# Expert layer of a two-block transformer kernel: 80 candidate sums, eight one-hot places, four operand places, pairs loaded two at a time

## The reference, cut to what matters

```python
q = (h @ w_q).reshape(B, S, 8, 2, 128)
s1, s2 = q[..., 0, :] . keys1, q[..., 1, :] . keys2        # 128 scores each, per token and head
v1, i1 = top_k(s1, 16);  v2, i2 = top_k(s2, 16)
cand = (v1[..., :, None] + v2[..., None, :]).reshape(..., 256)
sv, si = top_k(cand, 16)
experts = i1[si // 16] * 128 + i2[si % 16]                 # 128 picks per token, of 16384 experts
gates = softmax(sv)
a = h . u[experts];  act = gelu(a) * gates;  out = sum over picks of act * v[experts]
x = x + out
```

## Time and profile before

| | us |
|---|---|
| three runs | 2755.32, 2766.57, 2768.15 (median 2766.57) |
| profiled execution, its own time | 2760.16 |
| span from its first to its last instruction | 2758.3 |
| PE busy / DVE / POOL / ACT in the span | 2562.9 / 1672.7 / 1799.8 / 727.3 |
| stages that the change touches | about 1421 to 2752 of the span |

### The profile page before, as it was taken

The page is one execution under the profiler, slowest core; times in us unless marked ns, Lnnn a source line. Parts: engine busy times, 40 slices in busy tenths (PEclk is TensorE's granted clock), DMA queues, the critical chain, the costliest instruction groups (busy, mean ns, idle before and its releaser), DMA issues.

```text
span 2758.3 us, 36064 instructions
## 1 busy us (share of the span) xinstructions
PE 2562.9 (93%) x12644; PEld 2132.8 (77%) x12644; DVE 1672.7 (61%) x3126; ACT 727.3 (26%) x1297; POOL 1799.8 (65%) x1315
## 2 busy tenths in 40 slices
PE   3989799999989999999889989999999999999998
PEld 2866578888667676677768889999999977777776
DVE  5447532121245326463459998887878388878887
ACT  4148410000133323423210111111112123332332
POOL 2746557676733243374656558999986777887885
PEclk8989999999999999999999999999999999999999
DMA  6223212222311011121223337899997899999996
GB/s 243 92 84 138 107 64 104 92 93 101 112 46 46 31 67 60 46 104 65 78 98 109 109 140 263 312 350 348 349 333 258 320 321 325 328 325 326 324 328 246
DMA packets 160356, 502.55 MB, mean 182 GB/s; under 512 B 12273, under 2 KB 79473, under 8 KB 128753
## 3 DMA queue, kind: packets, MB, share of 16 engines
q1 hardware_dynamic: 96432, 311.98, 32.2%
q0 software_dynamic: 36864, 134.23, 13.1%
q10 hardware_dynamic: 26944, 54.85, 5.2%
HBM read 448.58 MB, written 52.43 MB: 182 GB/s over the span
## 4 chain that ended last, share of the span: by engine, by line
PE 54%; DVE 14%; POOL 12%; DMA 10%; issue 5%; ACT 4%; SPq 0%; ACTq 0%; DVEq 0%; POOLq 0%
PE banks L547 8%; PE banks L549 8%; PE banks L548 8%; POOL W_lo L409 7%; DMA arena<-gates_dram 5%; PE banks L675 3%; PE banks L693 2%; PE banks L905 2%; PE banks L907 2%; PE banks L906 2%; DMA B_lo_plain<-u_rows,arena 2%; PE banks L820 2%; POOL W_hi L417 2%; PE banks L651 2%; PE banks L822 2%
## 5 line engine op out<-in xcount | busy, mean ns | idle before, releaser
L409 POOL TENSOR_TENSOR W_lo<-raw,W_hi 128x2048 fp32r<-128x2048 f32 x127 | 587.1, 4623 | 55.6 <-ACT W_hi L1335 49.7
L434 POOL TENSOR_TENSOR W_lo<-raw,W_hi 128x512 fp32r<-128x512 f32 x376 | 494.0, 1324 | 0.0
L437 POOL TENSOR_TENSOR beat<-zero 128x1 f32<-128x1 f32 x94 | 19.8, 211 | 616.4 <-PE banks L695 215.4
L820 PE MATMUL banks<-A_hi,W_hi 128*128 128x384 f32 x1024 | 379.7, 371 | 17.5 <-ACT B_plain L1263 16.2
L822 PE MATMUL banks<-A_hi,W_lo 128*128 128x384 f32 x1024 | 345.5, 337 | 0.0
L821 PE MATMUL banks<-A_lo,W_hi 128*128 128x384 f32 x1024 | 344.5, 336 | 0.0
L905 PE MATMUL banks<-W_hi,B_hi 128*128 128x512 f32 x768 | 305.0, 397 | 30.1 <-DVE B_lo L1842 30.1
L907 PE MATMUL banks<-W_lo,B_hi 128*128 128x512 f32 x768 | 303.2, 395 | 0.0
L906 PE MATMUL banks<-W_hi,B_lo 128*128 128x512 f32 x768 | 303.2, 395 | 0.0
L547 PE MATMUL banks<-A_hi,W_hi 128*128 128x512 f32 x680 | 267.8, 394 | 4.9 <-issue 4.9
L549 PE MATMUL banks<-A_hi,W_lo 128*128 128x512 f32 x680 | 264.7, 389 | 0.0
(11 more groups left out here) (260 smaller groups left out, 5456.1 us busy)
## 6 DMA issues: line engine op xcount, KB each, us to landing
raw<-weights SPq DMA_DIRECT2D x241, 1024.0 KB
gelu_dram<-B_plain ACTq DMA_DIRECT2D x64, 384.0 KB
gates_dram<-arena ACTq DMA_DIRECT2D x48, 512.0 KB
arena<-gelu_dram SPq DMA_DIRECT2D x64, 384.0 KB
arena<-gates_dram SPq DMA_DIRECT2D x64, 384.0 KB
W_plain<-weights SPq DMA_DIRECT2D x4, 1024.0 KB, 16.1
X<-x_t SPq DMA_DIRECT2D x1, 2048.0 KB, 14.6
arena<-v_rows,arena POOLq DMA_INDIRECT x128, 8.1
```

Of the source, the lines that this page charges most:

```text
L409: pool.tensor_tensor(W_lo[:, s % 2, :], raw[:, s % 2, :], W_hi[:, s % 2, :].bitcast(F32), ALU.subtract)\
L434: return pool.tensor_tensor(W_lo[:, j, cols], raw[:, j, cols], W_hi[:, j, cols].bitcast(F32), ALU.subtract)
L820: mm(to, lh, rh, start=k == 0, stop=False)
```

## The change

Candidates: `CANDS = 80` in place of 256, made by three additions instead of one, and the place is turned back to row and column with eight more small DVE instructions. The exponential stands behind the gelu of the first slab of the picks stage, which has nine slabs instead of eight (the last block has three slabs behind its tokens instead of four); DVE does the place arithmetic before it waits for the exponential. Eight one-hot places instead of four. Gates of a block are stored two pieces a slab in the first four slabs of the next. In the last stage the operands have four places (high and low parts of slabs in `W` and `B`, of products in `A`), the products three; gelus and gates are loaded for two pairs in one DMA each (gates in pieces of 1024 bytes), with places for four pairs, asked between the two slabs; ACT does the operand of the pair before behind each slab, and DVE's order is low part, product of the pair after next, two adds.

```diff
-U_PICKS = 8
-U_BLOCKS = ((8, 0), (8, 0), (8, 0), (8, 0), (8, 0), (4, 4))
+HOTS = 8
+U_PICKS = 9
+U_BLOCKS = ((8, 0), (8, 0), (8, 0), (8, 0), (8, 0), (4, 3))
+        hot = [(hot_parts[:, j, 0, :], hot_parts[:, j, 1, :]) for j in range(4)] + \
+            [(A_plain[:, j, TD:T], A_lo_plain[:, j, TD:T]) for j in range(HOTS - 4)]
@@ SP
-                sp.dma_start(gelu_in[:, j, :], gelu_dram[s + j, :, :, :].rearrange("p i t -> p (i t)"))\
-                sp.dma_start(g_in[:, j, :].rearrange("p (q x) -> p q x", q=GB),
-                             g_dram[:, :, bass.ds(s * 2 + 2 * j, 2), :].rearrange("q p e t -> p q (e t)"))\
-            with sp.Fori(2, PAIRS - 1, 2) as s:
-                for j in range(2):
-                    value_slab(s, j)
-                    pair(s, j)
+            def two_pairs(s, d):
+                if s + d:
+                    if s:
+                        sp.wait_ge(act_ready, s + 2 * d - 2)
+                else:
+                    for j in range(2):
+                        sp.wait_ge(g_stored[j], 8 * STORES * GB)
+                for j in range(2):
+                    sp.wait_ge(gelu_stored[j], s * 8 + (16 * d + 16))
+                sp.dma_start(gelu_in[:, d, :].rearrange("p (s x) -> p s x", s=2), ...)
+                sp.dma_start(g_in[:, d, :].rearrange("p (q x) -> p q x", q=GB), ...)
+            two_pairs(0, 0)
+            two_pairs(0, 1)
+            for s in range(2, PAIRS, 2):
+                value_slab(s, 0)
+                if s + 2 < PAIRS:
+                    two_pairs((s + 2) // 4 * 4, (s + 2) // 2 % 2)
+                value_slab(s, 1)
@@ ACT
+            gelus(HEADS)
             take(small_ready)
             act.activation(eq[:, 512:1024], eq[:, 0:512], ACT.Exp).then_inc(small_done, 1)
-            for s in range(HEADS, HEADS + U_PICKS):
+            for s in range(HEADS + 1, HEADS + U_PICKS):
                 gelus(s)
-                        per_slab = STORES // with_tokens
-                        for part in range(per_slab * s, per_slab * s + per_slab):
+                        per_slab = STORES // 4
+                        for part in range(per_slab * s, min(STORES, per_slab * s + per_slab)):
                             store_gates(q - 1, part)
+            def high(p):
+                slab = p + N_MID + PAIRS
+                act.wait_ge(slab_loaded[slab % 2], 8 * (slab - slab % 2 + N_ADA - 4) + 16)
+                if p >= 4:
+                    act.wait_ge(slab_used, slab - 3)
+                act.activation(v_hi[p % 4], raw[:, slab % 2, :], ACT.Copy).then_inc(v_half, 1)
+            def operand(p):
+                act.wait_ge(act_ready, p + 1)
+                if p >= 4:
+                    act.wait_ge(slab_used, p + N_MID + PAIRS - 3)
+                act.activation(A_hi[:, 2 * (p % 4):2 * (p % 4) + 2, 0:TD], ...)
+            operand(0)
+            for p in range(2, PAIRS):
+                high(p)
+                operand(p - 1)
+            operand(PAIRS - 1)
@@ DVE
-                    dve.tensor_tensor(c.rearrange("p (i j) -> p i j", i=TOPK),
-                                      first.unsqueeze(2).to_broadcast([P, TOPK, TOPK]),
-                                      second_psum.unsqueeze(1).to_broadcast([P, TOPK, TOPK]),
+                    dve.tensor_tensor(c[:, 0:16], second_psum, first[:, 0:1].to_broadcast([P, TOPK]), ALU.add)
+                    dve.tensor_tensor(c[:, 72:80], first[:, 8:16], second_psum[:, 0:1].to_broadcast([P, 8]), ALU.add)
+                    dve.tensor_tensor(c[:, 16:72].rearrange("p (i j) -> p i j", i=7),
+                                      first[:, 1:8].unsqueeze(2).to_broadcast([P, 7, 8]),
+                                      second_psum[:, 0:8].unsqueeze(1).to_broadcast([P, 7, 8]),
                                       ALU.add).then_inc(work_free[b], 1)
+            dve.tensor_copy(row, iwu[:, 0, :])
+            step(dve.tensor_copy(place, iwu[:, 1, :]))
+            dve.scalar_tensor_tensor(out=last_rows, in0=row, scalar=9.0, in1=place, op0=ALU.is_equal, op1=ALU.mult)
+            dve.tensor_scalar(first_i, row, -1.0, 0.0, ALU.add, ALU.max)
+            step(dve.tensor_scalar(eights, row, 1.0, 8.0, ALU.is_equal, ALU.mult))
+            step(dve.tensor_tensor(first_j, place, eights, ALU.add))
+            dve.tensor_tensor(sel[:, 0, :, :].rearrange("p q s -> p (q s)"), last_rows, first_i, ALU.add)
+            dve.tensor_tensor(sel[:, 1, :, :].rearrange("p q s -> p (q s)"), first_j, last_rows, ALU.subtract)
-            step(dve.tensor_copy(sel.rearrange("p i q s -> p (i q s)"), iwu.rearrange("p i s -> p (i s)")))
+            for p in range(2):
+                product_of(p)
             for p in range(PAIRS):
-                product_of(p)
-                if p == 2:
+                low_of(p)
+                if p + 2 < PAIRS:
+                    product_of(p + 2)
+                if p == 1:
                     dve.wait_ge(x_rows_ready, 1)
-                if p >= 2:
-                    add_rows(p - 2)
-                low_of(p)
-            for p in range(PAIRS - 2, PAIRS):
-                add_rows(p)
+                if p >= 1:
+                    add_rows(p - 1)
+            add_rows(PAIRS - 1)
```

More of the change, by code:

```diff
@@ L21 @@
 TOPK = 16
+CANDS = TOPK + 7 * 8 + 8
 EPS = 1e-6
@@ L111, in build @@
         X = sb("X", [P, KD, T])
+        with nc.sbuf_tensor("A_plain", [P, KD, T], F32) as A_plain:
+            pass
         A_hi = sb("A_hi", [P, KD, T], F32R)
+        with nc.sbuf_tensor("A_lo_plain", [P, KD, T], F32) as A_lo_plain:
+            pass
         A_lo = sb("A_lo", [P, KD, T], F32R)
@@ L185, in build @@
         rest_a = at(7168, 2, KEYS)
-        cand = at(7424, 2, 256)
-        cand_rest = at(7936, 256)
+        cand = at(7424, 2, CANDS)
+        cand_rest = at(7936, CANDS)
         iota16 = at(8192, TOPK)
@@ L920, in outputs_of @@
                     last.then_inc(slab_used, 1)
-            with pe.Fori(0, PAIRS - 3, 2) as s:
-                for odd in range(2):
-                    outputs_of(s, odd)
-            outputs_of(PAIRS - 2, 0)
-            outputs_of(PAIRS - 2, 1, final=True)
+            with pe.Fori(0, PAIRS - 7, 4) as s:
+                for i in range(4):
+                    outputs_of(s, i)
+            for i in range(4):
+                outputs_of(PAIRS - 4, i, final=i == 3)
         @block.scalar
@@ L1327, in _ @@
             act.activation(dots, dots, ACT.Gelu).then_inc(dots_gelu, 1)
[L1329 to L1350 removed]
+            def high(p):
[8 more added lines that the diff above has]
+                    act.wait_ge(slab_used, p + N_MID + PAIRS - 3)
+                act.activation(A_hi[:, 2 * (p % 4):2 * (p % 4) + 2, 0:TD],
+                               prod[p % 3].rearrange("p (i t) -> p i t", i=2), ACT.Copy).then_inc(act_hi_ready, 1)
+            for i in range(2):
+                act.wait_ge(gelu_stored[i], 8 * PAIRS)
+            operand(0)
[3 more added lines that the diff above has]
+            operand(PAIRS - 1)
             act.wait_ge(x_rows_ready, QT)
@@ L1768, in _ @@
                 .then_inc(small_ready, 1)
+            iwu = iw.bitcast(U32)
+            eq3 = eq.rearrange("p (s j) -> p s j", j=TOPK)
+            eq4 = eq.rearrange("p (h s j) -> p h s j", h=HEADS, j=TOPK)
+            si = sum_iu.rearrange("p q h s -> p (q h s)")
+            dve.tensor_copy(iota_psum, iota)
+            step(dve.tensor_copy(iota16_psum, iota16))
+            dve.tensor_scalar(iwu[:, 0, :], si, 3, None, ALU.logical_shift_right)
+            step(dve.tensor_scalar(iwu[:, 1, :], si, 7, None, ALU.bitwise_and))
+            row, eights, last_rows = bank[4][:, :], bank[5][:, :], bank[1][:, :]
+            first_i, first_j, place = (at(512 * n, 512) for n in range(3))
+            dve.tensor_copy(row, iwu[:, 0, :])
[6 more added lines that the diff above has]
+            dve.tensor_tensor(sel[:, 1, :, :].rearrange("p q s -> p (q s)"), first_j, last_rows, ALU.subtract)
+            for q in range(QT):
+                ins = dve.tensor_copy(top_f[q], top_iu[:, q, :, :])
+            step(ins)
             take(small_done)
-            gsum = eq[:, 1024:1024 + QT * HEADS]
+            gsum = bank[0][:, 256:256 + QT * HEADS]
             step(dve.tensor_reduce(gsum, ex, AX, ALU.add))
```

110 lines of the change are left out of this document (43 added, 67 removed).

## The result

The changed kernel took 2726.44 us (median of four runs, 2722.96 to 2727.47), the kernel before 2765.64 beside it: a ratio of 0.986 [0.984, 0.988]. The profiled execution of the changed kernel took 2727.47 us, 32.7 less than the profiled one of before. The forecast was 2711: the sign was right, the gain was 39 us where 52 were forecast, and the time lies just beyond the slow end of the forecast's own range (2697 to 2726), inside the wide one (2690 to 2745).

The account below looks back on a forecast made before the run. PE was taken as the pace everywhere, with losses to DVE and DMA beside it. Gains of 9 (heads and picks), 4 (one-hots), 8 (passage) and 31 (last stage) sum to 52 us: 2762.6 to 2711, range 2697 to 2726.

Parts of the forecast that it names:

- the wide one: Whole kernel: time range of 2690 to 2745 us, taking in the POOL and DVE rival and most of the bounds.
- Heads: Heads stage: DVE tiles fall to 4.8 us, a head takes 21.7 us instead of 22.69, seven heads give 7 us.
- Picks: Pick stage: stall for the exponential goes, DVE ends the stage, one-hots begin at 1666.9; 9 us gained, bounds 2 to 12.
- One-hot stage: One-hot stage: earlier stores and eight places remove PE's stalls, limited by DMA; 4 us gained, between 14 lost and 12 gained.
- The stores' part: One-hot stage: storing two pieces a slab removes ACT's wait for a block's stores, behind three of PE's seven stalls.
- Passage: Last token's copy to PE's first last-stage matmul: 35 us instead of 43.1; 8 us gained, bounds 0 and 9.
- Last stage: Last stage: four places and products two pairs ahead hide late operands; 8.35 us a pair, 31 us gained, bounds 41 and 0.
- The signs set for this stage: Last stage: PE's low-part waits under 10 us, 534 us long, clock at 1.0, POOL over 85% busy.
- The rival of POOL and DVE holding each other: Last stage: blocked instructions lengthen every second or third pair; 8.84 us a pair, time 2742, chance 0.2.
- The rival of weights behind pairs: Last stage: slabs land late behind two pairs' loads; 10.1 us a pair, time 2823, slower, chance 0.06.
- Pieces: Last stage: gates' pieces of 1024 bytes cut DMA work by half of 0.8 us, from 8.1 to 7.7 us a pair.
- the rival that the piece size saves nothing: Last stage: DMA still needs 8.1 us a pair, so 8.4 us a pair and time 2713, chance 0.12.

Follow-up runs that it names:

- psum_all: Changed kernel with every small instruction of the pick stage given an operand or result in PSUM; 2714.92 us, 0.982 of the kernel before.
- hots_4: Changed kernel with four one-hot places instead of eight; 2724.98 us, 0.986 of the kernel before.
- last_only: Kernel before with only the last stage changed; 2730.55 us, 0.989 of the kernel before.
- front_only: Changed kernel with the last stage as it was before; 2754.14 us against 2761.76 for the kernel before, 0.997.
- gathers_4: `psum_all` with the third v slab asked after the first two pairs and v gathers one pair ahead instead of three; 2710.05 us, 0.981 of the kernel before.
- sums_256: Changed kernel with all 256 sums and the old place arithmetic; 2722.86 us, 0.987 of the kernel before.

## Why the prediction was right, and where its sizes were off

**Heads.** Right in kind. DVE's tile took 4.70 us (forecast 4.8), and the distance from head 1's last key to head 8's, 1432.68 to 1586.87, is 22.03 us a head, not 21.7: PE keeps all of its 0.73 us of idle time at a head. 4.6 us gained instead of 7.

**Picks.** This is the step that failed. The term was 9 us, with 2 to 12 as bounds, and 0.5 was measured; the one-hots began at 1677.10 (1675.4 without the later start of the heads), later than the 1674 that the prediction named as a sign of being wrong. The stall of the earlier trace rows went, and the eight instructions cost 4.9 us as worked out (1603.52 to 1608.43, forecast 4.8). But DVE's pick work took 73.4 us, not 68.0: the shift stood 4.0 us longer than its twin and L1830 2.0 longer than in `psum_all`. (The subtraction, 2.63 us before, took 1.74.) The prediction knew of such a block and kept it as the lower bound of 2 us; it counted on none beyond the one of before. DVE's pick work also started 2.2 us later, counted from head 1's first key, and the way from DVE's end to the first one-hot took 7.1 us instead of 6.2, at the lower clock: 8.5 us in all. Since DVE ends this stage, nothing hides what catches it.

**One-hot stage.** Its two parts were seen, at wrong sizes and one of them misplaced. The stores' part was real: ACT's wait is gone, and undoing it costs 6 us. Eight places do nothing (`hots_4`). PE stands 5.4 us instead of 8.7, and the slow first stretch (108 matmuls in 20 us where before had 126) costs 126 - 108 = 18 matmuls of 0.16 us, 2.9 us: the one pays for the other. In `psum_all` PE stood 1.91 us ahead of the stage and the clock fell all the same (107 matmuls), so that wait's length alone isn't the cause; what else sets it stays open. The DMA share of 0.92 says that DMA was not the limit that the prediction feared. The measured 0 rests on one trace of before: the same one-hot code took 471.6 us in `last_only`, 4 more, and 465.4 to 467.9 in the traces with the stores two a slab, so its gain is anywhere from nothing to 6 us, and the 4 of the forecast are neither shown nor refuted.

**Passage.** Right: 36.6 us for a forecast of 35. From the last token to the asking 25.7 (25.0), to the landing 8.0 (5 to 6), to PE 3.0 (3). The landing was the miss. `front_only`, which loads the pairs one by one, started its product 4.7 us behind the asking and had a passage of 34.6.

**Last stage.** Right in mechanism, as far as the parts of the edit were tried together: with products two ahead and four places DVE's low part is still caught behind POOL, in `gathers_4` at nearly every pair, and in steady running PE doesn't see it; a pair takes 8.2 us where 8.35 was forecast. The term was 27.4 for 31 because of the start: the first 50 us hold 167 matmuls where full rate is 221, 12 us lost to 7.6 us of waits and the clock behind them (0.81 in the window above). The prediction named one of the causes, ACT's operand behind the high part of the next slab, but spread it over the stage; it came at the start, together with DVE's low part caught for 3.7 us at either wait. The signs set for this stage were near: PE's waits for the low part 12.5 us and not under 10, POOL 84% busy and not 85. The rival of POOL and DVE holding each other didn't come as a pace: PE waited for the low part four times, 1.5 us in all, after 2230. The rival of weights behind pairs was there in its place but not in its price: two slabs landed 16 and 21 us after they were asked, at the start; from 2230 on the median is 5.4.

**Pieces.** Wrong, as shown above: the rival that the piece size saves nothing had it right. It was worth 0.4 us a pair of cover and entered no term of the sum, and the rival's time, 2713, is too near the forecast to tell them apart by time.

## What to carry to other kernels

Cutting elements on DVE by two thirds saved 9 us in the heads' tiles and lost as much where the new index arithmetic ran, because that stage ended on DVE: count what an edit adds in the stage where its engine is last, and look there for copies, casts, shifts and two-input instructions from SBUF to SBUF beside a long POOL instruction. Relieving one of them only hands the wait to the next; all must be moved. A deeper chain of operand places hides such waits at steady state and not in its first turn, before the places are filled: look there at what each engine's order puts ahead of the first operands.

## What the runs showed of the hardware that was not expected

- A DVE instruction of 0.23 us (cast 128x128) took 4.60 beside POOL's 4.62, and a shift of 0.41 took 4.45; the same with source or target in PSUM took 0.29 and 0.69 in `psum_all`. A reduction of 2.29 us from SBUF to SBUF inside POOL's 4.63 took its 2.29. PSUM is slower by 0.28 us for 128x512, and so the cheaper of the two here.
- The small additions over 56, 16 and 8 elements take 205, 174 and 152 ns. Between 16 and 56 an element costs 0.8 ns, so by estimate 6 of the 152 ns are for its 8 elements and the rest is fixed. MAX8 and FIND_INDEX8 take 245 and 235 ns over 80, 283 and 290 over 128.
- After 7.81 us without work PE ran at a granted clock of 0.50 for 12 us, through twenty-five short matmuls and the first 5 us of the one-hot stage; the kernel before, with idle times of 1.59, 0.58 and 1.32 us there, stayed at 1.00, and `psum_all`, with 1.91 and 1.06, fell. `sums_256`, with 1.57 and 1.06, fell to 0.64 in the first 5 us of its one-hots, and `last_only`, with 1.57, 0.31 and 1.06, stayed at 1.00: these idle times don't tell the two apart.
